# A state-space mixer rewritten: running sums spread by DMA, carried outputs scaled in VectorE, chunks unrolled

## The reference

```python
acum = cumsum(a, in a chunk)                        # a = dt * (-exp(a_log)), one number per token and head
decay = exp(where(causal, acum[l] - acum[s], -inf)) # 128 x 128 for each head
cb = einsum('lgn,sgn->lsg', C, B)
y_diag = einsum('lsge,sgep->lgep', cb * decay, x * dt)
states = einsum('lgn,lgep->gepn', B, x * dt * exp(acum[-1] - acum))
h_in[c + 1] = h_in[c] * exp(acum[-1]) + states[c]   # carried from chunk to chunk
y_off = einsum('lgn,gepn->lgep', C, h_in) * exp(acum)
y = (y_diag + y_off + d_skip * x) * silu(z), then an RMS norm over the channels
```

## Time and profile before

| | before |
|---|---|
| median of 3 runs | 3779.69 us (3773.59 to 3780.41) |
| span of the profiled execution | 3783.2 us |
| PE, DVE, ACT, POOL busy | 87%, 47%, 22%, 13% of the span |
| mean granted TensorE clock, whole span | 0.928 of full speed |
| state-space stage | about 735 to 1100 us of the span |

### The profile page before, as it was taken

The page is one execution under the profiler, slowest core; times in us unless marked ns, Lnnn a source line. Parts: engine busy times, 40 slices in busy tenths (PEclk is TensorE's granted clock), DMA queues, the critical chain, the costliest instruction groups (busy, mean ns, idle before and its releaser), DMA issues. The chain is left out here.

```text
span 3783.2 us, 40284 instructions
## 1 busy us (share of the span) xinstructions
PE 3277.9 (87%) x15052; PEld 2635.5 (70%) x15086; DVE 1777.2 (47%) x1732; ACT 845.9 (22%) x927; POOL 510.7 (13%) x459
## 2 busy tenths in 40 slices
PE   6899999777746956958987999999999799999599
PEld 4688888566534734746765888888888688787477
DVE  5761255477735234355516454454454532332443
ACT  4221111122214214221113111111111132321321
POOL 3000000078850320310003000000000000000110
PEclk8999999877878978978988999999999899999799
DMA  3222222122252070054231111111111253531432
GB/s 112 89 101 73 67 67 83 62 67 87 87 109 39 20 132 11 22 164 139 91 127 52 67 44 44 44 44 65 46 44 44 93 207 137 175 138 63 153 125 67
DMA packets 189830, 321.82 MB, mean 85 GB/s; under 512 B 10267, under 2 KB 90907, under 8 KB 184091
## 3 DMA queue, kind: packets, MB, share of 16 engines
q1 hardware_dynamic: 181590, 280.86, 22.5%
q0 software_dynamic: 8160, 39.88, 4.3%
HBM read 223.87 MB, written 96.77 MB: 85 GB/s over the span
## 5 line engine op out<-in xcount | busy, mean ns | idle before, releaser
L78 PE MATMUL up_ps<-up_h_hi,up_w_hi 128*128 128x512 f32 x1408 | 554.7, 394 | 38.1 <-DVE up_h_lo L184 37.3
L79 PE MATMUL up_ps<-up_h_lo,up_w_hi 128*128 128x512 f32 x1408 | 552.1, 392 | 0.0
L80 PE MATMUL up_ps<-up_h_hi,up_w_lo 128*128 128x512 f32 x1408 | 551.3, 392 | 0.0
L78 PE MATMUL inp_ps<-inp_h_hi,inp_w_hi 128*128 128x512 f32 x896 | 358.4, 400 | 31.3 <-DVE inp_h_lo L184 28.4
L79 PE MATMUL inp_ps<-inp_h_lo,inp_w_hi 128*128 128x512 f32 x896 | 353.5, 395 | 0.0
L80 PE MATMUL inp_ps<-inp_h_hi,inp_w_lo 128*128 128x512 f32 x896 | 352.8, 394 | 0.0
L78 PEld LDWEIGHTS up_ps<-up_h_hi,up_w_hi 128*128 128x128 f32 x1408 | 266.7, 189 | 100.7 <-issue 36.5
L1452 DVE TENSOR_TENSOR up_squares<-up_ps,up_rstd 128x2048 f32<-128x2048 f32 x44 | 100.9, 2292 | 439.8 <-PE up_ps L80 430.1
L80 PEld LDWEIGHTS up_ps<-up_h_hi,up_w_lo 128*128 128x128 f32 x1408 | 266.9, 190 | 55.9
L79 PEld LDWEIGHTS up_ps<-up_h_lo,up_w_hi 128*128 128x128 f32 x1408 | 267.0, 190 | 55.7 <-issue 0.5
L78 PE MATMUL down_banks<-down_a_hi,down_w_hi 128*128 128x512 f32 x704 | 276.8, 393 | 28.6 <-DVE down_a_lo L1583 27.0
(11 more groups left out here) (247 smaller groups left out, 5552.2 us busy)
## 6 DMA issues: line engine op xcount, KB each, us to landing
down_a_raw<-act SPq DMA_DIRECT2D x14, 2816.0 KB, 12.4
act<-up_room SPq DMA_DIRECT2D x22, 1024.0 KB, 4.6
up_room<-in_w_up_dram SPq DMA_DIRECT2D x42, 512.0 KB, 5.8
inp_room<-in_w_in_dram SPq DMA_DIRECT2D x26, 512.0 KB, 5.0
xbc<-inp_room SPq DMA_DIRECT2D x12, 1024.0 KB, 4.6
ssd_xbc<-xbc SPq DMA_DIRECT2D x16, 768.0 KB, 6.2
...
```

Source lines behind the costliest of these rows:

```text
L78: pe.matmul(out, w_hi, x_hi, start=first, stop=False)
L79: pe.matmul(out, w_hi, x_lo, start=False, stop=False)
L80: return pe.matmul(out, w_lo, x_hi, start=False, stop=last)
```

## The change

The mixer becomes a class `Ssd` whose engine programs are generators. `weave` merges such programs by the times they yield; here it gets one program, so each engine's order is the order of the code. The chunk loops are unrolled in Python, so no registers index the chunks.

- The running sums of all chunks and heads are made once, with token on the free axis, by two matmuls; their values and their exponentials are stored to DRAM (`cum_rows`, `e_rows`). For each chunk a DMA spreads 16 rows of sums to all 128 partitions, straight into the tile `m_t` (1 MB), and two DMAs spread the exponentials to `e_cum`, in the layout of the outputs (2 x 256 KB). `cumulate`, the second exponential and the parameter copies go.
- The difference is made in place, from SBUF, with a mask of -1e30 added by a minimum (L829 of the new kernel, `barred`); so C·B needs no mask, and the multiply reads it from PSUM (L844).
- The carried part has a PSUM tile `ps_o` of its own (8 matmuls of two heads each, with C unscaled). VectorE multiplies it by `e_cum` (L857) and adds the diagonal part `ps_y` (L861). `c_dec` goes.
- GpSimd adds that sum to d_skip·x (L722), then multiplies by z (L725). B is copied by ScalarE (L754).
- y, z and xde have one buffer; `ps_x` is one bank of PSUM, used in two halves in turn. The sums of squares over partitions are made for one output row, not 128.

```diff
-def ssd(nc, dt_raw, dt_bias, a_log, d_skip, z_t, xbc_t, mix_t, y_root):
...
+def weave(*programs):
+    due = [[next(p, None), p] for p in programs]
+    while any(t is not None for t, _ in due):
+        now = min((d for d in due if d[0] is not None), key=lambda d: d[0])
+        now[0] = next(now[1], None)
...
+    def sync(self, sp):
...
+        sp.dma_start(self.cum_rows.rearrange("(k p) t -> p k t", p=P), self.cum_t).then_inc(self.rows_st, 16)
+        sp.dma_start(self.e_rows.rearrange("(k p) t -> p k t", p=P), self.e_t).then_inc(self.rows_st, 16)
+        sp.wait_ge(self.rows_st, 32)
+        def load_cum(c):
+            if c >= 2:
+                sp.wait_ge(self.diag_mm, 2 * c - 2)
+            sp.dma_start(self.m_t[c % 2][:, :, :].rearrange("p h t -> p (h t)"),
+                         self.cum_rows[c * SH:(c + 1) * SH, :].rearrange("h t -> (h t)").unsqueeze(0).broadcast_to([P, SH * P])
+                         ).then_inc(self.cum_in[c % 2], 16)
+        def load_e(c):
+            if c >= 2:
+                sp.wait_ge(self.dy_s, c - 1)
+            rows = self.e_rows[c * SH:(c + 1) * SH, :].rearrange("(j e) t -> e j t", e=2)
+            for e in range(2):
+                sp.dma_start(self.e_cum[c % 2][64 * e:64 * e + 64], rows[e:e + 1].broadcast_to([64, SH // 2, P])
+                             ).then_inc(self.e_in[c % 2], 16)
...
+        for c in range(TT):
...
+            if c + 2 < TT:
+                load_x(c + 2)
+                load_cum(c + 2)
...
+            sp.wait_ge(self.y_out, c + 1)
+            sp.dma_start(self.y_t[:, :, c * P:(c + 1) * P], self.y[:, :, :]).then_inc(self.stored, 16)
+            if c + 1 < TT:
+                load_z(c + 1)
+            if c + 2 < TT:
+                load_e(c + 2)
...
+    def gpsimd(self, pool):
...
+        for c in range(TT):
+            pool.wait_ge(self.xdt_s, 2 * c + 2)
+            if c > 0:
+                pool.wait_ge(self.st_mm, 2 * c)
...
+            pool.tensor_tensor(self.xde[:, :, :], self.xdt[b][:, :, :],
+                               self.to_end[:, c].unsqueeze(2).broadcast_to([P, SH, SP_]), ALU.mult).then_inc(self.xde_s, 1)
+            if c > 0:
...
+                add_up(c - 1)
...
+            if c > 0:
+                pool.wait_ge(self.stored, 16 * c)
+                pool.wait_ge(self.sq_s, c)
+            pool.tensor_tensor(self.y[:, :, :], self.xbc[b][:, 0:INNER // P],
+                               self.d_col[:, :].unsqueeze(2).broadcast_to([P, INNER // P, P]), ALU.mult).then_inc(self.dx_s, 1)
...
+            if c > 0:
+                pool.wait_ge(self.state_s, 2 * c)
+                pool.wait_ge(self.off_mm, 2 * c)
+            pool.tensor_tensor(self.state[1 - b][:, :, :], self.state[b][:, :, :],
+                               self.chunk_decay[:, c].unsqueeze(2).broadcast_to([P, SH, SP_]), ALU.mult).then_inc(self.decayed_s, 1)
...
+            pool.wait_ge(self.y_add, 2 * c + 2)
+            pool.wait_ge(self.dx_s, c + 1)
+            pool.tensor_tensor(self.y[:, :, :], self.y[:, :, :], self.e_cum[b][:, :, :], ALU.add).then_inc(self.dy_s, 1)
...
+            pool.tensor_tensor(self.y[:, :, :], self.y[:, :, :], self.z[:, :, :], ALU.mult).then_inc(self.y_out, 1)
...
+    def scalar(self, act):
...
+        for c in range(TT):
...
+                act.wait_ge(self.seg_s, 2 * c + g + 1)
+                act.activation(self.m_t[b][:, heads], self.m_t[b][:, heads], ACT.Exp).then_inc(self.decay_s, 1)
...
+                    act.activation(self.b_tok[b][:, :, :], self.ps_b[:, 0:SG], ACT.Copy).then_inc(self.btok_s, 1)
+            if c > 0:
...
+                self.square(act, c - 1)
...
+    def vector(self, dve):
...
+        for c in range(TT):
+            for _ in self.tail(dve, c - 1, 0):
+                yield _
+            for _ in self.front(dve, c):
+                yield _
+            for _ in self.tail(dve, c - 1, 1):
+                yield _
...
+    def front(self, dve, c):
+        b = c % 2
+        for g in range(SG):
...
+            if g == 0:
+                dve.wait_ge(self.cum_in[b], 16 * (c // 2 + 1))
+            for h in range(g * self.HG, (g + 1) * self.HG):
+                last = dve.scalar_tensor_tensor(out=self.m_t[b][:, h], in0=self.m_t[b][:, h], scalar=self.neg_cum[:, c, h:h + 1],
+                                                in1=self.barred[:, :], op0=ALU.add, op1=ALU.min)
+            last.then_inc(self.seg_s, 1)
...
+            dve.wait_ge(self.turned_x, 2 * c + g + 1)
...
+            dve.tensor_tensor(self.xdt[b][:, heads], self.ps_x[:, :, :].rearrange("p a (h e) -> p (a h) e", e=SP_),
+                              self.dt[:, c, heads].unsqueeze(2).broadcast_to([P, self.HG, SP_]), ALU.mult).then_inc(self.xdt_s, 1)
+        for g in range(SG):
...
+            dve.wait_ge(self.decay_s, 2 * c + g + 1)
+            dve.wait_ge(self.btok_s, c + 1)
+            dve.tensor_tensor(self.m_t[b][:, heads], self.m_t[b][:, heads],
+                              self.ps_b[:, SG + g].unsqueeze(1).broadcast_to([P, self.HG, P]), ALU.mult).then_inc(self.m_s, 1)
+    def tail(self, dve, c, part):
...
+        if part == 0:
+            for g in range(SG):
...
+                dve.wait_ge(self.off_mm, 2 * c + g + 1)
+                dve.wait_ge(self.e_in[b], 32 * (c // 2 + 1))
+                dve.tensor_tensor(self.e_cum[b][:, tiles], self.ps_o[:, :, :], self.e_cum[b][:, tiles], ALU.mult).then_inc(self.off_s, 1)
...
+                dve.wait_ge(self.diag_mm, 2 * c + g + 1)
+                dve.wait_ge(self.off_s, 2 * c + g + 1)
+                dve.tensor_tensor(self.e_cum[b][:, tiles], self.ps_y[:, :, :], self.e_cum[b][:, tiles], ALU.add).then_inc(self.y_add, 1)
+        else:
+            for g in range(SG):
...
+                dve.wait_ge(self.st_mm, 2 * c + g + 1)
+                dve.wait_ge(self.decayed_s, c + 1)
+                dve.tensor_tensor(self.state[1 - b][:, heads], self.ps_x[:, :, :].rearrange("p a (h e) -> p (a h) e", e=SP_),
+                                  self.state[1 - b][:, heads], ALU.add).then_inc(self.state_s, 1)
...
+    def tensor(self, pe):
...
+        for k in range(2):
+            last = pe.matmul(self.ps_y[:, k], a_all[:, k * P:(k + 1) * P], self.upper[:, :], start=True, stop=True)
+        last.then_inc(self.cum_s, 1)
+        pe.matmul(self.ps_b[:, 0:2].rearrange("p a m -> p (a m)"), self.upper[:, :], a_all, start=True, stop=True).then_inc(self.cum_s, 1)
+        pe.matmul(self.ps_o[:, 0:2].rearrange("p a m -> p (a m)"), self.one[:, :], a_all, start=True, stop=True).then_inc(self.cum_s, 1)
...
+        for c in range(TT):
+            for _ in self.outputs(pe, c):
+                yield _
+            if c + 1 < TT:
+                for _ in self.turn(pe, c + 1):
+                    yield _
+            for _ in self.states(pe, c):
+                yield _
...
+    def outputs(self, pe, c):
+        b = c % 2
+        for g in range(SG):
...
+            if c + g > 0:
+                pe.wait_ge(self.off_s, 2 * c + g)
+            if c > 0:
+                pe.wait_ge(self.state_s, 2 * c)
...
+            for t in range(self.HALF):
+                last = pe.matmul(self.ps_o[:, t], state[:, g * self.HALF + t], self.xbc[b][:, XT - SG + g], start=True, stop=True)
+            last.then_inc(self.off_mm, 1)
...
+            pe.wait_ge(self.m_s, 2 * c + g + 1)
+            pe.wait_ge(self.xdt_s, 2 * c + g + 1)
+            if c + g > 0:
+                pe.wait_ge(self.y_add, 2 * c + g)
+            for h in range(self.HG):
+                e, head = h % 2, g * self.HG + h
+                last = pe.matmul(self.ps_y[64 * e:64 * e + 64, h // 2], self.xdt[b][:, head], self.m_t[b][:, head], start=True, stop=True)
+            last.then_inc(self.diag_mm, 1)
+    def states(self, pe, c):
+        b = c % 2
+        for g in range(SG):
...
+            pe.wait_ge(self.btok_s, c + 1)
+            pe.wait_ge(self.xde_s, c + 1)
+            pe.wait_ge(self.xdt_s, 2 * min(c + 2, TT))
+            if g == 1:
+                pe.wait_ge(self.state_s, 2 * c + 1)
...
+            pe.matmul(self.ps_x[:, :, :].rearrange("p a t -> p (a t)"), self.b_tok[b][:, g],
+                      self.xde[:, heads].rearrange("p h e -> p (h e)"), start=True, stop=True).then_inc(self.st_mm, 1)
...
-                pool.tensor_tensor(c_dec[g][:, :, :], e_cum[g][:, :, :],
-                dve.wait_ge(cum_mm, i * 4 + (b * 2 + g + 1))
-                    last = dve.tensor_scalar(seg[g][:, h], ps_cum[g][:, h], par_now[b][:, 1, g * HG + h:g * HG + h + 1],
-                        last = pe.matmul(ps_cum[g][:, h], a_now[b][:, part, g * HG + h:g * HG + h + 1].broadcast_to([P, P]),
-            with dve.Fori(0, TT // 2 - 1) as i:
...
+    cum_rows, e_rows = (scratch(name, (TT * SH, P)) for name in ("cum_rows", "e_rows"))
```

More of the change, by code:

```diff
@@ L543, in _ @@
             last.then_inc(dt_mm, 1)
-def ssd(nc, dt_raw, dt_bias, a_log, d_skip, z_t, xbc_t, mix_t, y_root):
-    HG = SH // SG
-    with Phase(nc, "ssd") as ph:
```

(43 more changed lines are left out.)

460 lines of the change are left out of this document (242 added, 218 removed).

## The result

The changed kernel takes 3816.41 us (median of 4 runs, 3810.02 to 3823.13), the kernel before 3780.05 us in the same comparison. The ratio is 1.0103, with a 95% interval of 1.0091 to 1.0115: 36 us slower, where 27 were forecast (3807, range 3762 to 3834).

A forecast was written before the change was run, and what follows sets the result against it. No engine is full; a loop of waits sets the period: GpSimd's 8.3 us behind 14 of VectorE and TensorE. 774.3 + 15 x 22.3 = 1108.8, with the end 1117.6 against 1090.64: +27, 3807 us, range 3762 to 3834.

The forecast's parts named there:

- Exclusion of the differences and GpSimd's last two instructions: VectorE's SBUF differences and GpSimd's L722 and L725 take turns, one instruction each; VectorE waits 4.7 us a period.
- `ps_x` in halves holds GpSimd: One bank in halves delays group 1's state matmul to D+13.95; GpSimd waits for it before `xde`, then needs 8.3 us.
- The period: One chunk of the loop takes 22.3 us, 2.1 above the 20.16 of the kernel before.
- half of L907's 1.95: Length taken for TensorE's state matmul of group 1, with 0.1 to start: from 12.85 to 13.95 in the period.
- 1.3 us of slack lies there, at either clock: TensorE's outputs with VectorE's last addition take 6.3 us, ending at 20.95, before GpSimd's next D at 22.3.
- With two heads to a matmul, half of the 16: TensorE's carried part: half of its 16 matmuls a chunk counted as removed work.
- The start: Before the loop: first difference at about 762.5 (now 759.32), outputs of chunk 0 at 774.3.
- The end: After the last period: add and multiply 4.9, square 1.06 + 0.2, squares 2.6; what follows TensorE's last sums stays as long.
- VectorE keeping its turn: Rival: VectorE holds the turn through a row of eight differences; 19.4 us a period, 3763 us; chance 0.14.
- no exclusion: Rival: differences and GpSimd do not block each other; 91 us less, about 3717 us; chance 0.07.
- late rows: Rival: the spread rows' DMA arrives late, missing by 4.8 us each period; +72, 3879 us; chance 0.06.
- the same loop at no change: Rival: same loop, small parts off by a microsecond or two; 20.3 a period, 3777 us; chance 0.11, including slightly faster.

The follow-up runs named there:

- mask_psum: Changed kernel with the mask of the differences copied once to PSUM and read there by L829, so each difference has one SBUF input: 3751.3 us.
- late_add: Changed kernel with GpSimd waiting before L722 until VectorE has made all differences of the next chunk: 3755.0 us.
- own_bank: Changed kernel with the new state's matmuls in two PSUM banks of their own, ahead of the next chunk's transposes: 3783.2 us.
- filler8: Changed kernel with six idle TensorE matmuls behind the transposes of group 0 and two behind those of group 1: 3804.0 us.
- combo: Changed kernel with the mask in PSUM, state matmuls in own banks ahead of the transposes, and the carried part in 16 one-head matmuls: 3703.8 us.

## Why the prediction was right, point by point

- **Exclusion of the differences and GpSimd's last two instructions: right.** For the first eight 6.35 us were measured in the chunk shown and 6.75 forecast (D to D+6.75), for the next eight 2.17 and 2.1. mask_psum and late_add, by two different means, take off 4.6 and 4.3 us a period, against 4.7 forecast for the blocking. The differences, unseen before, have the start distance of L804, 0.26.
- **`ps_x` in halves holds GpSimd: right.** L700 waits for the second state matmul 13 times of 13, 9.8 us. own_bank shows it, with the order that goes with it, worth 2.6 us.
- **The period: 22.3 forecast, 23.03 measured.** The term that was mis-sized is "half of L907's 1.95". In the earlier trace rows that was a matmul at the high level, taken for the changed kernel as it stood; there it takes 2.05, at the low level, in each of the 15 chunks. That is 1.05 too little. The other terms together were 0.45 too long, and GpSimd's wait before L722 adds 0.15 in the mean: 22.3 + 1.05 - 0.45 + 0.15 = 23.05. filler8 puts the matmul back to 1.10 in most chunks, and its period is near the forecast one; that it meets it is in part chance, since these other errors offset each other.
- **"1.3 us of slack lies there, at either clock": wrong.** The outputs took 6.7 to 8.0 us (8.0 from 947.25 to 955.25 in the chunk shown), not 6.3. The slack runs through 0.9, 0.4 and 0.0 and is missing by up to 0.5 in 4 of 13 chunks, where GpSimd waits at L722, the place that the prediction named as a sign of being wrong. The price of 0.23 for each of 24 matmuls was too low for the eight wide ones: four of them take 2.05 us at the low level (947.40), 0.51 each, and eight narrow ones 1.98, 0.25 each. By these prices all 24 take 8.1 us at the low level. They end sooner where the clock has risen in the second half.
- **"With two heads to a matmul, half of the 16" as a saving: wrong.** Four wide matmuls take 2.05 us at the low level, eight narrow ones 1.98. It cost little in the changed kernel while slack covered it; combo shows narrow ones better by 0.8 us a period once the outputs are on the path. Their own length gives about 0.15 of that (1.98 against 2.05 at the low level and 1.09 against 1.16 at the high one, for each group). The rest goes with an earlier rise of the clock, which no run isolates.
- **The start: 3.5 us too late.** The store to DRAM was issued at 752.64 and not 754.3; it and its wait took 2.4 us (next load at 755.02) for 2.7, and the load 4.4 for 5.5. Chunk 0's outputs ended at 770.7 and not 774.3.
- **The end: right within 0.2 up to TensorE's last sums** (8.6 us from the last L722, 8.8 forecast), but the stretch behind them did not stay as long: 7.4 us for 9.3. ScalarE's table load of 1.28 us, which stood behind the sums before (at 1096.45), now runs ahead of them (at 1122.20).
- **The sum:** -3.5 + 15 x 0.73 - 0.2 = +7.3, which is 1124.91 against 1117.6. The early start offsets a third of what the periods add, so the total is nearer than its terms.
- **Loads hidden: right.** Share 0.48, no waits. Whether the 64-partition transfers run at half rate isn't shown: the 256 KB pieces landed in 6.2 us, in a queue behind others.

The rivals: VectorE keeping its turn and no exclusion are both refuted by the 6.35 us beside an L722 of 2.38 us, late rows by the list of waits, and the same loop at no change by the period.
